# A router that selects its experts from masked logits, and a gather that waits for the plain selection only, in a two-block transformer kernel

## The reference, cut to what matters

```
grp = jnp.argmax(grp_logits, axis=-1)
p_grp = jnp.take_along_axis(jax.nn.softmax(grp_logits, axis=-1), grp[:, None], axis=-1)
in_grp = jnp.take_along_axis(exp_logits, grp[:, None, None], axis=1)[:, 0]
p_in, top_i = lax.top_k(jax.nn.softmax(in_grp, axis=-1), MOE_TOPK)
gate = p_grp * p_in / jnp.sum(p_in, axis=-1, keepdims=True)
expert = grp[:, None] * MOE_PER_GROUP + top_i
...
    return (jax.nn.silu(x_blk @ w_gate[e]) * (x_blk @ w_up[e])) @ w_down[e]
...
y = jax.ops.segment_sum(yb.astype(f32) * slot_w[:, None], slot_tok, num_segments=T + 1)[:T]
```

## Time and profile before

| what | value |
|---|---|
| median of 3 runs | 1366.22 us (1365.96 to 1366.57) |
| profiled execution, its own time | 1367.98 us |
| its span on the core | 1366.3 us |
| TensorE busy, share of the span | 1105.1 us, 81% |
| DVE busy | 525.6 us, 38% |
| ACT busy | 385.8 us, 28% |
| mean granted TensorE clock | 0.907 of full speed |
| mean rate of all transfers | 263 GB/s |

### The profile page before, as it was taken

How to read it: one execution, slowest core, us unless ns; L and a number is a source line. 1 busy time by engine, 2 the same in 40 slices (tenths; PEclk the granted TensorE clock), 3 DMA queues, 4 the chain that set the end, 5 groups by cost and what they waited for, 6 DMA issues and landing times.

```text
span 1366.3 us, 16138 instructions
## 1 busy us (share of the span) xinstructions
PE 1105.1 (81%) x6847; PEld 812.7 (59%) x6847; DVE 525.6 (38%) x581; ACT 385.8 (28%) x427; POOL 43.4 (3%) x69
## 2 busy tenths in 40 slices
PE   4699987765766566565648999989999998899997
PEld 0596565231313223131318999869988876899985
DVE  1644655010101101010125555455854695455543
ACT  1234632000000000000015444334544443444432
POOL 1100200000000000000000000000000120000000
PEclk9799995787878898898888999998999999899999
DMA  9965833799999999999977555463555354455430
GB/s 338 382 219 196 305 123 139 302 421 422 421 422 422 422 422 421 422 421 421 422 289 234 183 181 183 159 232 119 182 185 185 123 182 141 148 182 185 181 137 31
DMA packets 126099, 358.93 MB, mean 263 GB/s; under 512 B 9478, under 2 KB 55130, under 8 KB 101466
## 3 DMA queue, kind: packets, MB, share of 16 engines
q1 hardware_dynamic: 119552, 350.25, 67.0%
q10 hardware_dynamic: 6492, 7.88, 1.7%
HBM read 357.05 MB, written 1.05 MB: 262 GB/s over the span
## 4 chain that ended last, share of the span: by engine, by line
PE 61%; DMA 27%; DVE 5%; SPq 2%; ACT 2%; issue 1%; POOL 0%; DVEq 0%; ACTq 0%
PE psum L1675 16%; PE psum L1676 16%; PE psum L1677 16%; DMA ring<-in_moe_w_down_dram 14%; DMA ring<-in_moe_w_gate_dram 11%; PE psum L1865 3%; PE psum L1850 3%; DVE hn L1061 1%; SPq L575 1%; PE psum L1712 1%; DMA ring<-in_ada_w_dram 1%; SPq L549 1%; ACT hn L728 1%; PE psum L1720 1%; PE psum L1633 1%
## 5 line engine op out<-in xcount | busy, mean ns | idle before, releaser
L1328 DVE TENSOR_TENSOR wl<-ring,wh 128x2048 fp32r<-128x2048 f32 x102 | 234.3, 2302 | 246.0 <-ACT wh L878 245.8
L878 ACT ACTIVATE wh<-ring 128x2048 fp32r<-128x2048 f32 x102 | 195.2, 1915 | 310.2 <-PE psum L1677 309.7
L1675 PE MATMUL psum<-hTh,wh 128*128 128x256 f32 x832 | 237.3, 285 | 4.7 <-DVE hTl L1347 2.8
L1676 PE MATMUL psum<-hTl,wh 128*128 128x256 f32 x832 | 236.8, 285 | 0.0
L1677 PE MATMUL psum<-hTh,wl 128*128 128x256 f32 x832 | 236.6, 284 | 0.0
L1850 PE MATMUL psum<-ring,m_xT 128*32 128x512 f32 x1024 | 132.8, 672 | 69.2 <-DMA ring<-in_moe_w_up_dram 48.1
L1675 PEld LDWEIGHTS psum<-hTh,wh 128*128 128x128 f32 x832 | 160.8, 193 | 5.4 <-issue 5.3
L1676 PEld LDWEIGHTS psum<-hTl,wh 128*128 128x128 f32 x832 | 160.6, 193 | 0.0
L1677 PEld LDWEIGHTS psum<-hTh,wl 128*128 128x128 f32 x832 | 160.6, 193 | 0.0
L1865 PE MATMUL psum<-ring,m_hT 128*32 128x512 f32 x512 | 85.2, 826 | 60.5 <-DMA ring<-in_moe_w_down_dram 60.5
L1850 PEld LDWEIGHTS psum<-ring,m_xT 128*32 128x32 f32 x1024 | 40.3, 122 | 155.9 <-issue 155.9
(11 more groups left out here) (285 smaller groups left out, 1387.1 us busy)
## 6 DMA issues: line engine op xcount, KB each, us to landing
ring<-in_moe_w_gate_dram SPq DMA_DIRECT2D x64, 1024.0 KB, 18.8
ring<-in_moe_w_up_dram SPq DMA_DIRECT2D x64, 1024.0 KB, 12.8
ring<-in_moe_w_down_dram SPq DMA_DIRECT2D x64, 1024.0 KB, 18.7
ring<-in_ffn_w_in_dram SPq DMA_DIRECT2D x44, 1024.0 KB, 7.6
ring<-in_w_mix_in_dram SPq DMA_DIRECT2D x32, 1024.0 KB, 7.1
ring<-in_ada_w_dram SPq DMA_DIRECT2D x24, 1024.0 KB, 7.9
ring<-in_ffn_w_out_dram SPq DMA_DIRECT2D x20, 1024.0 KB, 6.3
ring<-in_sb_w_in_dram SPq DMA_DIRECT2D x12, 1024.0 KB, 16.1
```

What stands on the lines that cost most here:

```text
L878: a.activation(dst, src, ACT.Copy).then_inc(split_h, 1)
L1328: v.tensor_tensor(split_half(h, wl), raw_half(h), split_half(h, wh).bitcast(FP32), ALU.subtract)\
L1675: t.matmul(dst, sh, mh, start=first, stop=False, skip_group_check=True)
L1676: t.matmul(dst, sh, ml, start=False, stop=False, skip_group_check=True)
```

## The change

The router marks the groups that were not chosen and adds this mask to the expert logits in two steps fewer, and picks both experts from the masked logits themselves instead of from a softmax over them. The exponential over 64 elements per partition becomes one over 2, of the difference between the two chosen logits. It can be computed only when the second maximum is known, so the step that raises `r_diff` to 2 now stands behind the first choice and the second maximum. The gates follow from it in fewer steps, all of them behind `chosen`. `iota` counts from 1, so that `posm` needs no subtraction. TensorE's gather waits for `m_sel` only (`S.steps`), and the wait for `m_wsel` (`S.sel`) stands before its transposes.

```diff
--- before.py
+++ after.py
@@ -645,7 +645,7 @@
             for e in range(EG):
                 chain.link(g.affine_select(out=strip, in_=strip, compare_op=ALU.not_equal, fill=1.0, base=-CAP * e,
                                            pattern=[[0, P]], channel_multiplier=1))
-            g.iota(iota, pattern=[[1, EXPERTS]], base=0, channel_multiplier=0,
+            g.iota(iota, pattern=[[1, EXPERTS]], base=1, channel_multiplier=0,
                    allow_small_or_imprecise_dtypes=True).then_inc(consts, 1)
             g.iota(iotam, pattern=[[1, EXPERTS]], base=-64, channel_multiplier=0,
                    allow_small_or_imprecise_dtypes=True).then_inc(consts, 1)
@@ -826,7 +826,7 @@
             act.wait_ge(r_diff, 1)
             a.activation(route[:, 0:8], route[:, 0:8], ACT.Exp).then_inc(r_exp, 1)
             act.wait_ge(r_diff, 2)
-            a.activation(route[:, 64:128], route[:, 64:128], ACT.Exp).then_inc(r_exp, 1)
+            a.activation(route[:, 64:66], route[:, 64:66], ACT.Exp).then_inc(r_exp, 1)
 
             def expert_copies(it, S):
                 act.wait_ge(S.x_full, it + 1)
@@ -1196,14 +1196,13 @@
                 return flat if len(shape) == 1 else flat.rearrange("p (a b) -> p a b", a=shape[0])
 
             gl_e = rt(0, NT, GROUPS)
-            ex = rt(64, NT, EXPERTS)
+            e2 = rt(64, NT)
             logit = rt(128, NT, 36)
             gl, el = logit[:, :, 0:GROUPS], logit[:, :, GROUPS:]
-            ohg, t4, negm = rt(208, NT, GROUPS), rt(216, NT, GROUPS), rt(224, NT, GROUPS)
-            one_of = rt(240, NT, EXPERTS)
-            pm, t32 = rt(304, NT, EXPERTS), rt(368, NT, EXPERTS)
+            t4 = rt(216, NT, GROUPS)
+            masked, pm, t32 = (rt(at, NT, EXPERTS) for at in (240, 304, 368))
             oh1, oh2, chosen = rt(432, NT, EXPERTS), rt(496, NT, EXPERTS), rt(560, NT, EXPERTS)
-            gmax, gsum, emax, esum, idx, p1, p2, den = (rt(640 + 4 * n, NT) for n in range(8))
+            gmax, gsum, top1, top2, idx, p1, p2, den = (rt(640 + 4 * n, NT) for n in range(8))
             cmax = rt(700, 1)
 
             def wide(s, n):
@@ -1222,40 +1221,32 @@
             emptied(ins, ("router", 0))
             await_copied(dve, ("router", 0))
 
-            def first_max(dst, src, top, n, tmp):
-
-                link(v.tensor_reduce(top, src, AX, ALU.max))
+            def first_max(dst, src, top, n, tmp, op=ALU.is_equal):
+
+                index = iotam[:, 0:n].unsqueeze(1).to_broadcast([P, NT, n])
                 link(v.tensor_tensor(tmp, src, wide(top, n), ALU.is_equal))
-                link(v.tensor_tensor(tmp, tmp, iotam[:, 0:n].unsqueeze(1).to_broadcast([P, NT, n]), ALU.mult))
+                link(v.tensor_tensor(tmp, tmp, index, ALU.mult))
                 link(v.tensor_reduce(idx, tmp, AX, ALU.min))
-                link(v.tensor_tensor(dst, iotam[:, 0:n].unsqueeze(1).to_broadcast([P, NT, n]), wide(idx, n), ALU.is_equal))
+                link(v.tensor_tensor(dst, index, wide(idx, n), op))
 
             dve.wait_ge(consts, 11)
-            first_max(ohg, gl, gmax, GROUPS, t4)
+            link(v.tensor_reduce(gmax, gl, AX, ALU.max))
             v.tensor_tensor(gl_e, gl, wide(gmax, GROUPS), ALU.subtract).then_inc(r_diff, 1)
-            link(v.tensor_scalar(t4, ohg, -1.0, None, ALU.add))
-            link(v.tensor_scalar(negm, t4, 1e30, None, ALU.mult))
-            link(v.tensor_tensor(by_group(t32), by_group(el), wide8(negm), ALU.add))
-            link(v.tensor_reduce(emax, t32, AX, ALU.max))
-            v.tensor_tensor(ex, t32, wide(emax, EXPERTS), ALU.subtract).then_inc(r_diff, 1)
-            dve.wait_ge(r_exp, 1)
+            first_max(t4, gl, gmax, GROUPS, t4, ALU.not_equal)
+            link(v.scalar_tensor_tensor(by_group(masked), wide8(t4), -1e30, by_group(el), ALU.mult, ALU.add))
+            link(v.tensor_reduce(top1, masked, AX, ALU.max))
+            first_max(oh1, masked, top1, EXPERTS, t32)
+            link(v.scalar_tensor_tensor(pm, oh1, -2e30, masked, ALU.mult, ALU.add))
+            link(v.tensor_reduce(top2, pm, AX, ALU.max))
+            v.tensor_tensor(e2, top2, top1, ALU.subtract).then_inc(r_diff, 1)
+            first_max(oh2, pm, top2, EXPERTS, t32)
+            v.tensor_tensor(chosen, oh1, oh2, ALU.add).then_inc(r_sel, 1)
+
+            dve.wait_ge(r_exp, 2)
             link(v.tensor_reduce(gsum, gl_e, AX, ALU.add))
-            dve.wait_ge(r_exp, 2)
-            link(v.tensor_reduce(esum, ex, AX, ALU.add))
-            link(v.reciprocal(esum, esum))
-            link(v.tensor_tensor(one_of, ex, wide(esum, EXPERTS), ALU.mult))
-
-            link(v.tensor_tensor(by_group(pm), by_group(one_of), wide8(t4), ALU.add))
-            first_max(oh1, pm, p1, EXPERTS, t32)
-            link(v.scalar_tensor_tensor(pm, oh1, -4.0, pm, ALU.mult, ALU.add))
-            first_max(oh2, pm, p2, EXPERTS, t32)
-            v.tensor_tensor(chosen, oh1, oh2, ALU.add).then_inc(r_sel, 1)
-
-            link(v.tensor_tensor(den, p1, p2, ALU.add))
-            link(v.tensor_tensor(den, den, gsum, ALU.mult))
-            link(v.reciprocal(den, den))
-            link(v.tensor_tensor(p1, p1, den, ALU.mult))
-            link(v.tensor_tensor(p2, p2, den, ALU.mult))
+            link(v.scalar_tensor_tensor(den, e2, 1.0, gsum, ALU.add, ALU.mult))
+            link(v.reciprocal(p1, den))
+            link(v.tensor_tensor(p2, e2, p1, ALU.mult))
             link(v.tensor_tensor(gw, oh1, wide(p1, EXPERTS), ALU.mult))
             link(v.tensor_tensor(t32, oh2, wide(p2, EXPERTS), ALU.mult))
             link(v.tensor_tensor(gw, gw, t32, ALU.add))
@@ -1268,7 +1259,6 @@
                                          ALU.add, ALU.mult)
             emptied(ins, ("router", 1))
             await_copied(dve, ("router", 1))
-            link(v.tensor_scalar(posm, posm, -1.0, None, ALU.add))
 
             def expert_steps(g, it, S, steps):
 
@@ -1820,14 +1810,15 @@
             for name in [("T", 1, tt, i) for tt in range(NT) for i in range(2)] + [("router", 0), ("router", 1)]:
                 await_copied(pe, name)
 
-            def expert_group(it, S, first, landed):
+            def expert_group(it, S, first, landed, steps):
 
                 pe.wait_ge(S.acc, it + 1)
-                pe.wait_ge(S.sel, it + 1)
+                pe.wait_ge(S.steps, steps)
                 for c in range(KD):
                     for tt in range(NT):
                         t.matmul(psum[:, c // 4, P * (c % 4):P * (c % 4) + P], hn[:, tt, P * c:P * c + P],
                                  m_sel[:, tt].rearrange("p e s -> p (e s)"), start=(tt == 0), stop=(tt == NT - 1))
+                pe.wait_ge(S.sel, it + 1)
                 for tt in range(NT):
                     last = t.transpose(psum[:, 3, P * tt:P * tt + P],
                                        m_wsel[:, tt].rearrange("p e s -> p (e s)"), ident)
@@ -1876,7 +1867,7 @@
                 last.then_inc(S.c_full, 1)
 
             with pe.Fori(0, NEG) as g:
-                expert_group(g, main, NA, wa_in)
+                expert_group(g, main, NA, wa_in, g + 1)
             pe.wait_ge(r_done, 1)
             longest = pe.value_load(maxcount, min_val=0, max_val=T)
             with pe.If(longest > CAP):
@@ -1884,7 +1875,7 @@
                 with pe.Fori(0, ROUNDS - 1) as r:
                     with pe.If(longest > (r + 1) * CAP):
                         with pe.Fori(0, NEG) as g:
-                            expert_group(r * NEG + g, over, 0, over_in)
+                            expert_group(r * NEG + g, over, 0, over_in, r * (NEG + 1) + g + 2)
                     pe.end_ifs()
             pe.end_ifs()
             pe.wait_ge(main.acc, NEG + 1)
```

## The result

The changed kernel takes 1368.44 us in the median of 20 runs (1363.17 to 1370.38), the kernel before 1365.32 in the median of 20 (1360.15 to 1366.57; the three runs known at the time of the prediction gave 1366.22). The ratio is 1.0026, with a 95% interval of 1.0016 to 1.0037: **slower by 0.26%, some 3.5 us** (the means, 1364.49 and 1368.01, differ by that; the medians differ by 3.1). The two profiled executions hide it: their spans are 1366.3 and 1366.4. Single executions of either kernel scatter over some 7 us, so the two traces are compared stretch by stretch, from a common event on.

What follows compares the result with a forecast made beforehand. Transfers bound the experts' loop, and TensorE's order of work up to the first refill sets its start. The terms 0.95 - 0.24 - 0.54 = +0.17 us on the median 1366.22 gave 1366.4 us, range 1365.0 to 1370.8.

Steps and rivals of the forecast that it cites:

- What bounds it: Transfers pace the experts' loop (DMA share 1.01); whatever moves SP's first refill, at 247.21, moves everything behind it equally.
- The selection on DVE: ACT's release comes 1.08 us later, `chosen` 2.16 us earlier; that gain is worth nothing while TensorE reaches the counts later.
- The pause: On TensorE ahead of both sums: L1720 waits for ACT's later first copy, adding 0.95 us.
- `posm` and the gather: On the path to the first gather: dropping L1271 saves 0.24 us, waiting for `m_sel` only saves 0.54 us.
- The clock: Open term in TensorE's sums: if the rise stays at 227.5, the total is -0.36 us; range -0.4 to +1.0.
- the rival: The pause keeps TensorE at 1.2 GHz through both sums: +3.1 us, 1369.3 us; chance 0.41, with 0.32 above 1368.95.
- The two faster rivals: TensorE was waiting for `chosen` (1363.3 us, chance 0.05); the loop's trips wait for TensorE (1362.6 us, chance 0.02).

Runs made afterwards that it cites:

- e8: The kernel before with only two spare copies added on ACT ahead of the copy L1720 waits for: 1.0023 of the kernel before, median 1368.99 us.
- e9: The e8 kernel with one more TensorE product, which nobody reads, in the pause: 1.0011 of the kernel before, median 1365.54 us.
- after_look1: The changed kernel executed and profiled once more, with nothing changed: 1370.33 us.
- after_look2: The changed kernel executed and profiled a third time, with nothing changed: 1371.87 us.
- the last experiment: As e5, but DVE copies both units and adds their bias row, and TensorE's two bias products are gone: 0.9980 of the kernel before, median 1361.85 us.
- e5: The changed kernel with TensorE's last conditioning unit right behind the one before, both ACT copies before both exponentials: 1.0001 of the kernel before, median 1364.21 us.
- e3: The changed kernel with the old slots and the gather's old wait, so only the router's part: 1.0039 of the kernel before, median 1369.51 us.

## Why the prediction was right or wrong

- *What bounds it, and that the moment of the first refill carries to the end:* right, as far as single traces can show. The DMA share in the loop is 1.01 in both; from the first refill to the end it is 1119.1 before, 1120.6 after, 1118.9 with the pause alone and 1120.8 in the fastest kernel, while that moment moves by 10 us between them. The scatter of this rest, 2.7 us over all traces, is as large as the effects that are asked for.
- *The selection on DVE:* right. L1241 starts 3.13 behind the first maximum (219.31 to 222.44; forecast 3.13), and `chosen` ends 4.45 behind it (forecast 4.46). Worth nothing for the path there, as forecast, since TensorE came later.
- *The pause:* forecast 0.95, measured 1.00. In the execution of the router's part alone, with its early rise, it is 1.52, within what the prediction allowed for (up to 0.8 more).
- *`posm` and the gather:* forecast 0.24 and 0.54, measured 0.78 together (2.29 to 1.51).
- *The clock:* **here it failed.** The forecast of +0.17 us, made the likeliest at 0.52, took it that the pause costs its length and that the rise to 2.4 GHz in the sums stays. The runs showed that it does not: the pause alone gives four pairs at 2.0 us, and filling it gives the rise back. From the router's products to the start of the gather, the stretch that the sum is about, it is 16.77 us before (218.52 to 235.29) and 20.01 after (215.34 to 235.35): 3.24 more, where the forecast had 0.17 and the rival 3.07. So the rival had the mechanism and the price. Its argument was in the rows: the rise fell into the very pair that was to be delayed. What I set against it, that L1712's work ahead of the pause might still count, I had no row for; e8 and e9 decide it for a pause of 1 us behind work at the low level. The range given, 1365.0 to 1370.8, holds the measured 1368.44 because it was drawn around this rival too, not because the forecast of 1366.4 was near.
- *The price of the slow case in the time* is less well known than in the stretch. In the changed kernel's profile 1.5 of the 3.24 us came back, since the level rose 2.8 us into the gather and not 5.9, and the gather took 5.14 and not 6.61; after_look1 is alike, and in after_look2 the rise came 6.0 us into it, the gather took 6.66 and nothing came back. The prediction had only the reverse of this, a gather that gets slower. The three intervals of the router are 1.75, 1.81 and 3.29 above that of the kernel before, and the times differ by 2.2 to 5.1 us (the interval of the ratio). That the medians differ by 3.1, as the rival has it, is therefore in part luck.
- *A reading:* the prediction has the level fall in 231.00 to 231.50. That stretch is at 0.50 throughout; the fall is at the end of the one before it, near 230.9. No term rests on it.
- *The two faster rivals* did not occur. That `chosen` is on the path became true only in the last experiment, after L1712 (3.6 us at 1.2 GHz) and both products of the bias row (2.1 us at 2.4 GHz) were out of the way.
- The sentence from the Trainium skill's page "TensorE: Matmul & The Clock Gate" (Part 1, "What's actually happening"), that throttled is the default and activity releases it, agrees with e8 and e9: a product that nobody reads made the stretch 3.2 us shorter. In e5 activity by itself was not enough: TensorE was busy without a pause from 217.20 to the end of the counts, and the granted clock stayed at 0.50. That the point of the rise differs from run to run agrees too: in three executions of the changed kernel it came 2.8, 2.9 and 6.0 us into the gather.

## What to carry to other kernels

A step moved later on one engine is to be followed through every in-order queue that it heads: here DVE's chain was shortened, but the step that frees ACT went back by 1.1 us, and two unrelated copies stood behind it. Where TensorE works at 1.2 GHz and its rise comes soon behind, a pause of 1 us may cost not its length but all the work up to the next rise, as in e8; where the rise is ahead of the pause, as in the profile of e3, even 1.5 us did not bring the level down. So read the granted clock in the stretch ahead of the place and ask whether the rise falls behind the new pause. With a scatter of 7 us between executions, a stretch with a common start and end tells more than two spans. And two single traces can be compared in the clock only if the level stood alike ahead of the place; a piece of code that both share shows whether it did.

## What was not expected of the hardware

A useless product of 1.65 us makes the following four pairs take 4.4 us in place of 8.0. And taking 3.6 us of work off TensorE ahead of the sums (e5) brought the router's interval down by 2.25 us only: TensorE was never idle, and yet the level did not come up, and the sums took 8.0 us and not 5.1. That work taken away can come back in the clock of the work behind it had not been in any term of the prediction.
